# Attention of the first block: values stationary in two column halves, sums of weights by GpSimd and ones, results by feature

## The chip, the core and the metric

The kernel runs on one core of one Trainium2 chip. The core has five engines that run side by side and meet by semaphores: TensorE (matrix products, results in PSUM, eight banks of 128 partitions by 512 4-byte floats), VectorE, ScalarE, GpSimd (which reads and writes SBUF alone) and SyncE, which issues transfers. The metric is the time of one execution in microseconds (us) on the device; less is better.

## The reference, cut to what matters

The program is a block with retention and sparse attention, then a second block of two layers, in 4-byte floats, 512 tokens, width 1024. The change touches only the sparse attention of the first block. It has 8 query heads in 2 groups of 4 that share keys and values of 64 features, and three sides: compressed keys (31), selected keys and keys in a window. With 512 tokens the 16 best key blocks are all of the 8 that exist, so the second side takes in every earlier token, as the third does. For each block of 128 queries:

```python
p_cmp = masked_softmax(jnp.einsum('bgrtd,bgnd->bgrtn', qb, kc_g), valid_c)
o_cmp = jnp.einsum('bgrtn,bgnd->bgrtd', p_cmp, vc_g)
...
p_slc = masked_softmax(s_slc, smask).reshape(B, G, R, QB, topk, SLC_BLOCK)
o_slc = jnp.einsum('bgrtks,bgtksd->bgrtd', p_slc, vg)
...
p_win = masked_softmax(jnp.einsum('bgrtd,bgsd->bgrts', qb, kwb), wmask)
o_win = jnp.einsum('bgrts,bgsd->bgrtd', p_win, vwb)
...
out = gates[:, :, 0] * to_bshd(o_cmp) + gates[:, :, 1] * to_bshd(o_slc) + gates[:, :, 2] * to_bshd(o_win)
```

The result stands beside the retention's and is multiplied by the output projection.

## The kernel before

The stage has eight **units** (list `nsa`): four tiles `qt` of 128 queries by two groups `g`. A unit has one **block** of compressed keys (`s=0`) and two (`s=1, 2`) for each tile `kt` of 128 keys up to its own, 3, 5, 7 or 9 blocks, 48 in all. `first` is the number of a unit's first block, counted over all units.

For a block, `block_scores` writes scores of 128 keys by 4 heads x 128 queries into PSUM bank 4 or 5: a product of the high parts, a mask (compressed block and last key tile), a product with the rest parts, which also subtracts the largest score. ScalarE turns them into weights, `pr`, in a ring of four buffers. `block_values` then takes each head's 128x128 weights as the stationary operand and moves 65 columns of values, of which the last is one, so that the sum of the weights comes with the products. A product of plain 4-byte floats is two records of TensorE in the trace, one of the marked type (fp32r) is one. The sums of a unit's 12 heads and sides stand by token in banks 6 and 7.

The largest scores come from **rounds** (`best_round`): for the unit two further on, TensorE multiplies queries and keys in banks 2 and 3 in turn, VectorE reduces each over the keys (`largest`), `lowest` makes the shifts, `turn_low` transposes them in bank 1, and `spread_low` puts them among the rest queries `ql`. A round must wait until the one two before it is reduced.

At a unit's end VectorE (`unit_result`) bounds the sums, divides by them times the gates (`gates` holds one plus an exponential, so a division is the gate), multiplies all 12 results (`term`), and adds the three sides into `by_token`. After two units (one token tile) `turn_tokens` transposes four 128x128 tiles into bank 0 or 2, ScalarE writes the high part (`tokens_high`), VectorE the rest (`tokens_low`), in `h_hi` and `h_lo`, tiles 4 to 7. There is no scheduler: each engine runs its instructions in the order in which its function writes them. In the last two units TensorE also multiplies four tiles for the retention (`ret_widen`, its diagonal by `ret_diagonal` and its end by `ret_finish` on VectorE). VectorE splits two weight panels (`low(OUT1)`, `low(OUT1 + 1)`) before unit 5's results. ScalarE's halves of these splits (`split(33)`, `split(34)`) stand ahead of the first exponential.

After the stage the output projection takes tiles 0 to 3 (retention) of two panels, then tiles 4 to 7 (attention) of them: 24 and 24 products of 512 columns. GpSimd has nothing in the stage. A later attention of the kernel, in the second block (records L986 and L999, additions L588 on GpSimd, transposes L2696 on VectorE), works on two heads at a time in the two column halves of the array.

## Time and profile before

| | |
|---|---|
| median of 3 runs | 1913.14 us (1908.67 to 1914.05) |
| profiled execution | 1912.61 us |
| its span, first to last instruction | 1910.8 us |
| TensorE busy | 1856.8 us, 97% |
| VectorE, ScalarE, GpSimd busy | 1139.7, 735.9, 175.7 us |
| mean granted clock of TensorE | 0.991 |

"Busy" of TensorE counts each matmul to its modelled end, which lies beyond the start of the next; distances between starts tell more. A row of the timeline gives start, duration, engine, line, operation, operands, shapes and, in brackets, the idle time before it and what ended it. The granted clock is 1.00 at 2.4 GHz and 0.50 at 1.2 GHz.

### The profile page before, as it was taken

The numbers are of one execution on the slowest core, as the hardware profiler recorded it, in microseconds if no ns is written. First come the engines' busy times: TensorE is split into PE (matmuls) and PEld (weight loads), VectorE is DVE, ScalarE is ACT, GpSimd is POOL, SyncE is SP. The second block draws the span as 40 slices with busy tenths as digits, with TensorE's granted clock in tenths as the row PEclk, the third lists the DMA queues.
The fourth block names the chain that finished last, engine by engine and source line by source line (L and its number), as shares of the span: only waits on it lengthen the run. The fifth ranks groups of instructions, "written<-read, shape, count | busy, mean of one in ns | idle before, by whom it ended". The sixth has DMA issues, their size and how long they took to land.

```text
span 1910.8 us, 24681 instructions
## 1 busy us (share of the span) xinstructions
PE 1856.8 (97%) x8914; PEld 1513.4 (79%) x8914; DVE 1139.7 (60%) x1625; ACT 735.9 (39%) x1077; POOL 175.7 (9%) x181
## 2 busy tenths in 40 slices
PE   8999989999999999999999999999999999999998
PEld 6788778888888887887788888888666688888887
DVE  7767654784774778777543434476777554334344
ACT  6355222542432444554432322343544342323232
POOL 0020000300000011010000000002467300000000
PEclk9999999999999999999999999999999999999999
DMA  6232013233333332311333333332110133333332
GB/s 211 89 126 73 1 44 112 66 95 95 98 90 107 91 120 78 100 56 45 94 91 97 99 99 94 93 98 88 56 32 25 45 89 99 99 99 92 95 99 88
DMA packets 48216, 165.68 MB, mean 87 GB/s; under 512 B 5376, under 2 KB 7424, under 8 KB 48000
## 3 DMA queue, kind: packets, MB, share of 16 engines
q1 hardware_dynamic: 46512, 161.27, 27.8%
q10 hardware_dynamic: 1616, 3.22, 0.5%
q8 instruction: 56, 0.92, 0.2%
q14 instruction: 32, 0.26, 0.0%
HBM read 162.38 MB, written 2.10 MB: 86 GB/s over the span
## 4 chain that ended last, share of the span: by engine, by line
PE 86%; DVE 8%; ACT 2%; issue 2%; POOL 1%; DMA 0%; SPq 0%; DVEq 0%; ACTq 0%; POOLq 0%
PE ps L625 26%; PE ps L627 25%; PE ps L626 25%; PE ps L883 2%; PE ps L986 2%; DVE w_lo L2077 1%; POOL x L538 1%; ACT w_hi L1441 1%; PE ps L847 1%; PE ps L1241 1%; DVE tmp L2114 1%; PE ps L956 1%; PE ps L868 0%; DVE qk_c L2799 0%; PE ps L816 0%
## 5 line engine op out<-in xcount | busy, mean ns | idle before, releaser
L1441 ACT ACTIVATE w_hi<-raw 128x1024 fp32r<-128x1024 f32 x280 | 296.7, 1060 | 779.5 <-PE ps L627 779.3
L625 PE MATMUL ps<-h_hi,w_hi 128*128 128x512 f32 (+1 forms) x1288 | 509.3, 395 | 10.1 <-DVE w_lo L2352 7.2
L626 PE MATMUL ps<-h_lo,w_hi 128*128 128x512 f32 (+1 forms) x1288 | 500.0, 388 | 0.0
L627 PE MATMUL ps<-h_hi,w_lo 128*128 128x512 f32 (+1 forms) x1288 | 499.9, 388 | 0.0
L2077 DVE TENSOR_TENSOR w_lo<-raw,w_hi 128x1024 fp32r<-128x1024 f32 x280 | 345.0, 1232 | 120.6 <-ACT w_hi L1441 119.0
L625 PEld LDWEIGHTS ps<-h_hi,w_hi 128*128 128x128 f32 x1288 | 243.2, 189 | 64.6 <-DVE w_lo L2352 7.2
L627 PEld LDWEIGHTS ps<-h_hi,w_lo 128*128 128x128 f32 x1288 | 243.0, 189 | 50.6
L626 PEld LDWEIGHTS ps<-h_lo,w_hi 128*128 128x128 f32 x1288 | 243.1, 189 | 49.5 <-issue 2.0
L625 PE MATMUL ps<-hid_hi,w_hi 128*128 128x512 f32 (+1 forms) x716 | 273.6, 382 | 1.8 <-DVE w_lo L2077 0.9
L627 PE MATMUL ps<-hid_hi,w_lo 128*128 128x512 f32 (+1 forms) x716 | 272.6, 381 | 0.0
L626 PE MATMUL ps<-hid_lo,w_hi 128*128 128x512 f32 (+1 forms) x716 | 272.6, 381 | 0.0
L2292 DVE TENSOR_TENSOR x<-x,ps 128x512 f32<-128x512 f32 (+2 forms) x82 | 55.3, 674 | 191.6 <-PE ps L627 191.4
L625 PEld LDWEIGHTS ps<-hid_hi,w_hi 128*128 128x128 f32 x716 | 134.6, 188 | 28.9 <-DVE w_lo L2077 2.1
L627 PEld LDWEIGHTS ps<-hid_hi,w_lo 128*128 128x128 f32 x716 | 134.6, 188 | 25.9
L626 PEld LDWEIGHTS ps<-hid_lo,w_hi 128*128 128x128 f32 x716 | 134.6, 188 | 25.7
L2990 DVE SCALAR_TENSOR_TENSOR ev<-ps,tmp 128x512 f32<-128x512 f32 x64 | 44.1, 691 | 155.8 <-PE ps L627 152.8
L511 POOL TENSOR_TENSOR r<-r,small 128x2 f32<-128x2 f32 x6 | 4.2, 700 | 887.1 <-DVE r L2181 887.1
L1736 ACT ACTIVATE pr<-ps 128x512 f32<-128x512 f32 x48 | 27.9, 599 | 76.7 <-PE ps L873 76.6
L506 POOL TENSOR_TENSOR r<-r,small 128x4 f32<-128x4 f32 x8 | 8.1, 1012 | 516.2 <-DVE r L2127 516.2
L2684 DVE TENSOR_REDUCE mla_negm<-ps 128x1 f32<-128x512 f32 x64 | 41.2, 685 | 15.5 <-PE ps L956 14.8
L2732 DVE TENSOR_TENSOR ev<-ps,tmp 128x512 f32<-128x512 f32 x44 | 30.4, 692 | 28.8 <-PE ps L627 27.3
L625 PE MATMUL ps<-w_hi,h_hi 128*128 128x512 f32 (+1 forms) x128 | 47.0, 367 | 0.1
(412 smaller groups left out, 2522.8 us busy)
## 6 DMA issues: line engine op xcount, KB each, us to landing
raw<-in_panels SPq DMA_DIRECT2D x295, 512.0 KB, 3.6
x_in<-in_x SPq DMA_DIRECT2D x8, 256.0 KB, 5.7
x<-in_x ACTq DMA_DIRECT2D x1, 2048.0 KB, 8.4
out<-y SPq DMA_DIRECT2D x16, 128.0 KB, 1.8
first<-in_first SPq DMA_DIRECT2D x1, 1568.0 KB, 11.5
raw<-in_panels SPq DMA_DIRECT2D x2, 256.0 KB, 4.5
second<-in_second ACTq DMA_DIRECT2D x1, 512.0 KB, 3.7
small<-in_small ACTq DMA_DIRECT2D x1, 328.0 KB, 4.0
```

Of the source, the lines that this page charges most:

```text
L625: nc.tensor.matmul(out, a[0], b[0], start=start, stop=False)
L626: nc.tensor.matmul(out, a[0], b[1], start=False, stop=False)
L627: return nc.tensor.matmul(out, a[1], b[0], start=False, stop=stop)
L883: last = nc.tensor.matmul(ps[:, 6 + n // 6, n % 6 * 65:n % 6 * 65 + 65], pr[:, m % 4, h * P:(h + 1) * P], v, start=w["kt"] == 0 and n in ( ...
L986: last = nc.tensor.matmul(ps[64 * a:64 * a + 64, pair_bank(p), cols_of(half)], mla_v[:, kt, n, :], weights_tile(n, kt)[:, cols_of(half)], ...
L1441: nc.scalar.activation(w_high(panel, i), raw[:, panel % 4, :], ACT.Copy).then_inc(w_hi_ready, 1)
L1736: nc.scalar.activation(pr[:, m % 4, :], ps[:, 4 + m % 2, :], ACT.Exp, scale=0.125).then_inc(block_exp, 1)
L2077: signal(V.tensor_tensor(w_low(panel, i), raw[:, panel % 4, :], w_high(panel, i).bitcast(F32), ALU.subtract), w_lo_ready, wait=False)
L2292: signal(V.tensor_tensor(x[:, k, at], x[:, k, at], bank, ALU.add), done)
L2684: signal(V.tensor_reduce(mla_negm[:, n % 2, t:t + 1], ps[:, 2 + t % 2, :], AX.X, ALU.max, negate=True), mx_done, wait=False)
L2732: signal(V.tensor_tensor(src, bank, inv_b, ALU.mult), tile_out)
L2990: signal(V.scalar_tensor_tensor(ev[:, k % 4, :], bank, 0.0, inv_b, ALU.max, ALU.mult), tile_out, wait=False)
```

## The change

The values (64 columns now) become the stationary operand, and a block's weights move: heads 0 and 1 (256 columns) through the array's first 64 columns, heads 2 and 3 through the other 64. The result stands by feature, features of two heads in the two halves of 128 partitions. The compressed side goes to bank 0, the two others to bank 6 or 7 by unit. The rows of `w_out` are put in the order that fits, on the host's side.

The sums of weights come in another way. For the compressed block, `block_values` also multiplies its weights by ones. For the other sides GpSimd adds the weights of all key tiles (`add_block`), and `unit_sums` multiplies the totals by ones, in bank 1. The gates are spread once (`spread_gates`). VectorE has two functions for results: `compressed_result`, and `unit_result` for the other two sides; each transposes the sums in 32x32 squares, takes the larger of them and a bound times the gate value, the reciprocal, transposes back, and multiplies. GpSimd adds the three terms (`unit_add`) and, after ScalarE's rounding (`unit_rounded`), subtracts (`unit_rest`). For the last unit VectorE does both (`last_sum`). The transposes by token go.

The order is one list of 48 blocks, taken in pairs: the scores of two blocks (with their rounds), then the value products of the two before them; the sums of unit n come after the pair that holds block 2 of unit n+1. `pr` has six buffers. ScalarE's splits of the two panels go to unit 5, VectorE's to units 6 and 7. `x` is still loaded when ScalarE is through with the stage.

```diff
-            pr = sb("pr", [P, 4, S], F32, cc)
-            by_token = sb("by_token", [P, 2, 4, P], F32, cc)
-            term = sb("term", [P, 3, 4, 64], F32, cc)
+            pr = sb("pr", [P, PROBS, S], F32, cc)
+            term = sb("term", [P, 2, 3, 256], F32, cc)
+            unit_out = sb("unit_out", [P, 2, 256], F32, cc)
...
+        def add_block(m):
+            u, b = flat[m]
+            n, w = u["n"], u["blocks"][b]
+            if w["s"] == 0 or w["kt"] == 0:
+                return
+            if w["kt"] == 1 and n >= 2:
+                pool.wait_ge(unit_totals, n)
+            pool.wait_ge(block_exp, m + 1)
+            total = block_sum(n, w["s"])
+            nc.gpsimd.tensor_tensor(total, prob(m - 2) if w["kt"] == 1 else total, prob(m), ALU.add).then_inc(unit_added, 1)
+            pool.wait_ge(unit_added, last_add(m))
+        def unit_add(n):
+            pool.wait_ge(sum_taken, n + 1)
+            pool.wait_ge(compressed_taken, n + 1)
+            if n >= 2:
+                pool.wait_ge(unit_low, n - 1)
+            t = unit_out[:, n % 2, :]
+            nc.gpsimd.tensor_tensor(t, term[:, n % 2, 0, :], term[:, n % 2, 1, :], ALU.add).then_inc(unit_sum, 1)
+            pool.wait_ge(unit_sum, 2 * n + 1)
+            nc.gpsimd.tensor_tensor(t, t, term[:, n % 2, 2, :], ALU.add).then_inc(unit_sum, 1)
+            pool.wait_ge(unit_sum, 2 * n + 2)
...
+        def unit_rest(n):
+            pool.wait_ge(unit_high, n + 1)
+            hi, lo = unit_tiles(h_hi, nsa[n]), unit_tiles(h_lo, nsa[n])
+            nc.gpsimd.tensor_tensor(lo, unit_out[:, n % 2, :].rearrange("p (j q) -> p j q", j=2), hi.bitcast(F32), ALU.subtract).then_inc(unit_low, 1)
+            pool.wait_ge(unit_low, n + 1)
...
+        for m in range(NSA_BLOCKS):
+            for u in nsa[1:]:
+                if m == u["first"] + 5:
+                    unit_add(u["n"] - 1)
+            add_block(m)
+            for u in nsa[1:]:
+                if m == u["first"] + 10:
+                    unit_rest(u["n"] - 1)
+        unit_rest(NSA_UNITS - 2)
...
+        def unit_sums(u):
+            n = u["n"]
+            if u["qt"]:
+                pe.wait_ge(unit_added, adds_before[n + 1])
+            pe.wait_ge(unit_taken, bank_one["taken"])
+            pe.wait_ge(low_spread, bank_one["spread"])
+            for s in (1, 2):
+                moving = block_sum(n, s) if u["qt"] else prob(u["first"] + s)
+                for a in range(2):
+                    last = nc.tensor.matmul(ps[64 * a:64 * a + 64, 1, cols_of(s - 1)], ones[:, 0:64], moving[:, cols_of(a)],
+                                            start=True, stop=True)
+            last.then_inc(unit_totals, 1)
+            bank_one["taken"] = n + 2
...
+            if b == 0 and n:
+                pe.wait_ge(compressed_taken, n)
+            if b == 0 and n == NSA_UNITS - 1:
+                pe.wait_ge(mix_ready, 2)
+            if b == 1 and n >= 2:
+                pe.wait_ge(sum_taken, n - 1)
-            for h in range(4):
-                n = 4 * w["s"] + h
-                last = nc.tensor.matmul(ps[:, 6 + n // 6, n % 6 * 65:n % 6 * 65 + 65], pr[:, m % 4, h * P:(h + 1) * P], v,
-                                        start=w["kt"] == 0 and n in (0, 6), stop=w["last"], skip_group_check=True)
+            bank, at = (6 + n % 2, cols_of(w["s"] - 1)) if w["s"] else (0, cols_of(0))
+            for a in range(2):
+                last = nc.tensor.matmul(ps[64 * a:64 * a + 64, bank, at], v, prob(m)[:, cols_of(a)], start=w["kt"] == 0 and w["s"] < 2,
+                                        stop=w["last"], skip_group_check=True)
+            if b == 0:
+                for a in range(2):
+                    last = nc.tensor.matmul(ps[64 * a:64 * a + 64, 0, cols_of(1)], ones[:, 0:64], prob(m)[:, cols_of(a)], start=True,
+                                            stop=True, skip_group_check=True)
...
-        for n, u in enumerate(nsa):
-            count = len(u["blocks"])
-            block_scores(u, 0)
-            block_scores(u, 1)
-            if n + 1 < NSA_UNITS:
-                turn_low(nsa[n + 1])
-            block_values(u, 0)
-            if n and n % 2 == 0:
-                turn_tokens(n // 2 - 1)
-            for b in range(1, count):
-                if b + 1 < count:
-                    block_scores(u, b + 1)
-                if n + 2 < NSA_UNITS:
-                    for r in rounds_at(n, b):
-                        best_round(nsa[n + 2], r)
+        for m in range(2):
+            block_scores(*flat[m])
+        turn_low(nsa[1])
+        for m in range(0, NSA_BLOCKS, 2):
+            for k, (u, b) in enumerate(flat[m:m + 2]):
+                if m + 2 + k < NSA_BLOCKS:
+                    block_scores(*flat[m + 2 + k])
+                if u["n"] + 2 < NSA_UNITS:
+                    for r in rounds_at(u["n"], b):
+                        best_round(nsa[u["n"] + 2], r)
+            for u in nsa[2:]:
+                if m == turned_at(u["n"]):
+                    turn_low(u)
+            for u, b in flat[m:m + 2]:
                 block_values(u, b)
+            if m == 0:
+                spread_gates()
+            for u, b in flat[m:m + 2]:
+                n = u["n"]
+                if b == 2 and n:
                 if n >= NSA_UNITS - 2 and b in (2, 5):
-                    if n == NSA_UNITS - 2 and b == 2:
-                        pe.wait_ge(mix_ready, NT - 1)
+                    pe.wait_ge(compressed_taken, n + 1)
                     ret_widen(2 * (n - NSA_UNITS + 2) + b // 3)
-        turn_tokens(NT - 1)
+        unit_sums(nsa[-1])
...
+        for m in range(NSA_BLOCKS):
+            act.wait_ge(block_s, m + 1)
+            if m >= PROBS:
+                u, b = flat[m - PROBS]
+                act.wait_ge(block_pv, m - PROBS + 1)
+                if last_add(m - PROBS):
+                    act.wait_ge(unit_added, last_add(m - PROBS))
+                elif b:
+                    act.wait_ge(unit_totals, u["n"] + 2)
+            nc.scalar.activation(prob(m), ps[:, 4 + m % 2, :], ACT.Exp, scale=0.125).then_inc(block_exp, 1)
+            for u in nsa[1:]:
+                if m == u["first"] + 8:
+                    unit_rounded(u["n"] - 1)
+            if m in (nsa[-3]["first"] + 2, nsa[-3]["first"] + 4):
+                split(OUT1 + (m - nsa[-3]["first"]) // 2 - 1)
...
+        def compressed_result(u):
+            n, w = u["n"], w24[:, 0:8]
+            totals, shares = tmp[:, 1, 0:256], tmp[:, 1, 256:S]
+            dve.wait_ge(block_pv, u["first"] + 1)
+            link(V.transpose(totals, ps[:, 0, 256:S]))
+            link(V.scalar_tensor_tensor(w, totals[:, 0:256:32], 1e-30, gate_at(u, 0, 1)[:, 0, :], ALU.max, ALU.mult))
+            link(V.reciprocal(w, w))
+            link(V.transpose(shares, w.unsqueeze(2).to_broadcast([P, 8, 32])))
+            if n >= 2:
+                dve.wait_ge(unit_sum, 2 * n - 2)
+            signal(V.tensor_tensor(term[:, n % 2, 2, :], ps[:, 0, 0:256], shares, ALU.mult), compressed_taken, wait=False)
...
         def unit_result(u):
-            n, g, qt = u["n"], u["g"], u["qt"]
-            by = ps[:, 6:8, 0:390].rearrange("p b (i d) -> p b i d", d=65)
-            halves = w12[:].rearrange("p (b i) -> p b i", b=2)
-            sides = w12[:].rearrange("p (s h) -> p s h", s=3)
+            n, w = u["n"], w24[:, 8:24]
+            totals, shares = sq[:, 0, :], sq[:, 1, :]
+            dve.wait_ge(unit_totals, n + 2)
+            signal(V.transpose(totals, ps[:, 1, :]), unit_taken)
+            link(V.scalar_tensor_tensor(w.rearrange("p (s c) -> p s c", s=2), totals[:, 0:S:32].rearrange("p (s c) -> p s c", s=2), 1e-30,
+                                        gate_at(u, 1, 3), ALU.max, ALU.mult))
+            link(V.reciprocal(w, w))
+            link(V.transpose(shares, w.unsqueeze(2).to_broadcast([P, 16, 32])))
             dve.wait_ge(block_pv, u["first"] + len(u["blocks"]))
...
+        V.tensor_scalar(gates[:, :, 0:24], gates[:, :, 0:24], 1e38, 1.0, ALU.min, ALU.add).then_inc(gates_ready, 1)
+        spread_low(nsa[1])
+        for m in range(0, NSA_BLOCKS, 2):
+            for u, b in flat[m:m + 2]:
+                if u["n"] + 2 < NSA_UNITS:
+                    for r in rounds_at(u["n"], b):
+                        largest(nsa[u["n"] + 2], r)
+                    if b == len(u["blocks"]) - 1:
+                        lowest(nsa[u["n"] + 2])
+            for u in nsa[2:]:
+                if m == turned_at(u["n"]):
+                    spread_low(u)
...
+            for u, b in flat[m:m + 2]:
+                n = u["n"]
+                if b == 0:
+                    compressed_result(u)
+                if b == 2 and n:
+                    unit_result(nsa[n - 1])
+                if n == NSA_UNITS - 2 and b == 1:
+                    ret_diagonal(0)
-            if n + 2 < NSA_UNITS:
-                lowest(nsa[n + 2])
-            if n == NSA_UNITS - 3:
-                ret_diagonal(0)
-                low(OUT1)
-                low(OUT1 + 1)
+                if n >= NSA_UNITS - 2 and b == 7:
+                    low(OUT1 + n - NSA_UNITS + 2)
```

The start of unit 4 on TensorE, before (`kcs`, `ks` keys, `qs` queries, `vc`, `nv` values, `negm` shifts):

```order
L868 MATMUL ps<-qs0,kcs0 128x512 [waits block_exp,low_spread]
L871 MATMUL ps<-masks 128x512
L873 MATMUL ps<-ql0,kcl0 128x512
L868 MATMUL ps<-qs0,ks00 128x512 [waits block_exp,low_spread]
L873 MATMUL ps<-ql0,kl00 128x512
L859 MATMUL ps<-small,negm 12x128 [waits low_spread,low_ready]
L883 MATMUL ps<-vc,pr 128x65 [waits sum_taken,block_exp]
L883 MATMUL ps<-vc,pr 128x65 x3
```

and now, from the scores of its third block on:

```order
L960 MATMUL ps<-qs0,ks00 128x512 [waits block_exp,low_spread]
L965 MATMUL ps<-ql0,kl00 128x512
L910 MATMUL ps<-ks00,qs0 128x512 [waits best_done]
L914 MATMUL ps<-masks 128x128
L979 MATMUL ps<-pr,vc 64x256 [waits compressed_taken,block_exp]
L979 MATMUL ps<-pr,vc 64x256
L983 MATMUL ps<-pr,small 64x256 x2
L979 MATMUL ps<-pr,nv 64x256 [waits sum_taken,block_exp]
L979 MATMUL ps<-pr,nv 64x256
```

The first value products now stand behind the scores of two further blocks, they no longer wait for the unit before (`compressed_taken` is of unit 3's first block, `sum_taken` of unit 2), and two blocks' products are together.

The results of unit 3 on VectorE, before:

```order
L2607 TENSOR_SCALAR negm<-mx 128x12 [waits best_done]
L2624 TENSOR_SCALAR w<-ps 128x12 [waits block_pv]
L2625 TENSOR_TENSOR w<-w,gates 128x12 [waits dve_step]
L2626 RECIPROCAL w<-w 128x12 [waits dve_step]
L2627 TENSOR_TENSOR term<-ps,w 128x768 [waits dve_step]
L2632 TENSOR_TENSOR by_token<-term 128x4x64 [waits sum_taken]
L2633 TENSOR_TENSOR by_token<-by_token,term 128x4x64 [waits dve_step]
```

and now, with the compressed results of unit 4 ahead of them and reductions (L2706) between:

```order
L2731 STREAM_TRANSPOSE tmp<-ps 128x256 [waits block_pv]
L2732 SCALAR_TENSOR_TENSOR w<-tmp,gate_w 128x8 [waits dve_step]
L2733 RECIPROCAL w<-w 128x8 [waits dve_step]
L2734 STREAM_TRANSPOSE tmp<-w 128x256 [waits dve_step]
L2737 TENSOR_TENSOR term<-ps,tmp 128x256 [waits unit_sum,dve_step]
L2706 TENSOR_REDUCE mx<-ps 128x1 [waits best_ready] x3
L2719 TENSOR_TENSOR ql<-ps,small 12x512 [waits low_turned]
L2744 STREAM_TRANSPOSE sq<-ps 128x512 [waits unit_totals]
L2745 SCALAR_TENSOR_TENSOR w<-sq,gate_w 128x16 [waits unit_taken]
L2747 RECIPROCAL w<-w 128x16 [waits dve_step]
L2748 STREAM_TRANSPOSE sq<-w 128x512 [waits dve_step]
L2752 TENSOR_TENSOR term<-ps,sq 128x512 [waits unit_sum,block_pv,dve_step]
```

One set of results became two, each with two transposes, and reductions stand behind both.

GpSimd's last instructions in the stage, where it had none (`ev` holds the totals):

```order
L561 TENSOR_TENSOR ev<-pr 128x512 [waits block_exp,unit_totals,unit_added]
L571 TENSOR_TENSOR unit_out<-term 128x256 [waits compressed_taken,unit_low,sum_taken,unit_added]
L573 TENSOR_TENSOR unit_out<-unit_out,term 128x256 [waits unit_sum]
L561 TENSOR_TENSOR ev<-ev,pr 128x512 [waits block_exp,unit_sum]
L561 TENSOR_TENSOR ev<-ev,pr 128x512 [waits block_exp,unit_added] x3
L580 TENSOR_TENSOR h_lo<-unit_out,h_hi 128x2x128 [waits unit_high,unit_added]
```

Unit 6's results stand ahead of the last four additions of unit 7, for which TensorE's last sums wait.

## Rows read from the trace of the kernel before

**Rows 1.** page, part 4: chain that ended last, shares by engine.

```profile
PE 86%; DVE 8%; ACT 2%; issue 2%; POOL 1%; DMA 0%; SPq 0%; DVEq 0%; ACTq 0%; POOLq 0%
```

**Rows 2.** busy time by engine in windows: units 0+1, 2+3, 4, 5, 6, 7.

```profile
core 0: us, PE busy (x) PEld busy (x) DVE busy (x) ACT busy (x) POOL busy (x), PEclk, DMA share, GB/s
177.10:194.10 17.00, 15.62 (x116) 12.75 (x116) 11.21 (x25) 3.93 (x7) 0.00 (x0) 1.00 0.00 1
194.10:218.30 24.20, 22.51 (x161) 18.01 (x161) 16.00 (x36) 6.23 (x12) 0.00 (x0) 1.00 0.01 2
218.30:233.30 15.00, 14.39 (x102) 11.46 (x103) 9.22 (x19) 4.58 (x9) 0.00 (x0) 1.00 0.00 0
233.30:252.40 19.10, 15.62 (x98) 12.25 (x98) 11.60 (x21) 4.07 (x7) 0.00 (x0) 0.91 0.08 24
252.40:270.00 17.60, 16.95 (x102) 14.33 (x102) 10.31 (x19) 5.72 (x10) 0.00 (x0) 0.90 0.09 35
270.00:286.80 16.80, 14.08 (x96) 12.04 (x97) 8.91 (x17) 4.21 (x8) 0.00 (x0) 1.00 0.19 65
```

**Rows 3.** groups of lines by form, 160 to 300 us: | busy us, mean ns | idle, releaser.

```profile
L883 PE MATMUL ps<-vc,pr 128*128 128x65 f32 x64 | 9.0, 284 | 7.1 <-DVE term L2627 5.9 <-ACT pr L1736 1.2
...
L2627 DVE TENSOR_TENSOR term<-ps,w 128x768 f32<-128x768 f32 x8 | 7.7, 957 | 0.3
...
L2632 DVE TENSOR_TENSOR by_token<-term 128x256 f32<-128x256 f32 x8 | 3.4, 425 | 0.3
...
L2642 DVE TENSOR_TENSOR h_lo<-ps,h_hi 128x512 fp32r<-128x512 f32 x4 | 2.7, 686 | 4.2 <-ACT h_hi L1727 4.2
```

**Rows 4.** timeline of TensorE, two plain blocks of unit 6.

```profile
260.25 0.48 PE L868 MATMUL ps<-qs,ks 128*128 128x512 f32 x1
260.57 0.40 PE L873 MATMUL ps<-ql,kl 128*128 128x512 f32 x1
260.81 1.00 PE L883 MATMUL ps<-nv,pr 128*128 128x65 f32 x8
261.61 0.47 PE L868 MATMUL ps<-qs,ks 128*128 128x512 f32 x1
```

**Rows 5.** timeline of TensorE, column halves in the later attention.

```profile
1408.62 1.08 PE L999 MATMUL ps<-tmp,small 128*64 128x256 f32 x8 [0.30 <-issue]
1409.50 0.38 PE L986 MATMUL ps<-c_raw,mla_v 128*64 128x256 f32 x1
...
1411.05 0.38 PE L986 MATMUL ps<-ev,mla_v 128*64 128x256 f32 x1
1411.36 0.50 PE L625 MATMUL ps<-q_hi,k_hi 128*128 128x512 f32 x1
1411.70 0.40 PE L626 MATMUL ps<-q_lo,k_hi 128*128 128x512 f32 x1
...
1416.27 0.61 PE L956 MATMUL ps<-k_hi,q_hi 128*128 128x512 f32 x2
1416.82 0.43 PE L986 MATMUL ps<-c_raw,mla_v 128*64 128x256 f32 x1
```

**Rows 6.** timelines of TensorE and VectorE: starts of units 3 and 6, the end.

```profile
206.36 0.41 PE L883 MATMUL ps<-vc,pr 128*128 128x65 f32 x2 [0.50 <-DVE term L2627]
...
248.40 2.36 DVE L2077 TENSOR_TENSOR w_lo<-raw,w_hi 128x1024 fp32r<-128x1024 f32 x2
...
252.44 0.41 PE L883 MATMUL ps<-vc,pr 128*128 128x65 f32 x2 [3.50 <-DVE term L2627]
...
286.40 0.66 PE L891 MATMUL ps<-small,by_token 128*128 128x128 f32 x4 [2.72 <-DVE by_token L2633]
```

**Rows 7.** groups by form, whole span, GpSimd and VectorE.

```profile
L538 POOL TENSOR_TENSOR x<-x,tmp 128x256 f32<-128x256 f32 x32 | 26.9, 870 | 6.4 <-DVE tmp L2196 6.3
L588 POOL TENSOR_TENSOR tmp<-tmp,c_raw 128x512 f32<-128x512 f32 x16 | 23.8, 1485 | 5.1 <-ACT c_raw L1717 4.2
...
L2696 DVE STREAM_TRANSPOSE sq<-ps 128x512 f32<-128x512 f32 x8 | 5.7, 717 | 6.0 <-PE ps L999 5.9
```

149 lines of the change are left out of this document (79 added, 70 removed).

## The prediction

> **What bounds the kernel now.** I read the chain of work that ended last first: 86% of the span is TensorE's [rows 1], so a microsecond counts only where TensorE works or waits. The change touches one stage, the block attention from 177.1 to 286.8 us. The windows by unit [rows 2] show TensorE busy in most of each unit, but that figure hides short waits, since a matmul's shown duration overlaps the next one's. So I work from distances between starts. VectorE is busy 67.3 us in the six windows (11.2 + 16.0 + 9.2 + 11.6 + 10.3 + 8.9), ScalarE 28.7 us, GpSimd not at all. The stage is TensorE's, with VectorE second, and TensorE waits for VectorE in places that can be named [rows 6]. The granted clock is 1.00 but in two windows, 0.91 over 19.1 us and 0.90 over 17.6 us [rows 2]: some 3.5 us at the lower of its two levels (1.2 for 2.4 GHz) in each, the second behind a wait of 3.5 us [rows 6]. Each cost half of that, 1.7 us.
>
> **Products of a block.** Now four heads' weights are each the stationary operand and 65 columns of values move: eight records (each product in 4-byte floats is two). From one block's scores (260.25) to the next one's (261.61) is 1.36 us: 0.32 to the second score product, 0.24 to the first value product, 0.80 to the next scores [rows 4]. There are 48 blocks in 24 pairs, so a pair of unmasked ones takes 2.72 us. The new form has no row in this stage, but a later attention of this kernel uses it: 64 columns stationary, 256 moving, the two column halves alternating. Eight such records, which is what two blocks will need, take 0.88 us (1408.62 to 1409.50), and the return to full-width products costs 0.31 and then 0.34 us between starts, where 0.24 is usual [rows 5]. Entering costs 0.32 (1416.27 has two records in the list, so I take 0.55 from the first, less one usual step of 0.23) [rows 5]. A new pair: 0.34 + 0.24 + 0.24 for its four score products, 0.32 to enter, 0.67 from the first to the last of eight value records (sixteen take 1.55, 1409.50 to 1411.05, less 0.88), 0.31 to leave: 2.12 us. That saves 0.60 a pair, 14.4 us for 24. The bounds: without the switching cost (0.26 a pair, namely 0.10 + 0.08 + 0.08 over usual steps) 20.6 us; if each block of a pair paid it, 8.2 us.
>
> The page TensorEngine Tiling (Array Packing) of the Trainium skill (section Key Properties) says that changing the tiling mode, not merely the tile, drains the engine, and it speaks against this change. By that rule, the trace agrees: 0.31 and 0.34 us on the way out [rows 5]. With it the products save 14.4 us, without it 20.6.
>
> **What TensorE gets in addition.** Sums of weights no longer come with a 65th column. Per unit: four records with ones for the compressed block, half of 0.88, and eight for the two summed sides, 0.88. Eight units: 3.5 + 7.0 = 10.5 us [rows 5]. Once, the gates are spread with eight records of 96 columns, at the 0.11 us of a record of 65 (0.80/7) [rows 4] 0.9 us; at twice that 1.8. What goes: four times four transposes, at 0.11 us a record as well, 1.8 us. TensorE's own work falls by 14.4 - 10.5 - 0.9 + 1.8 = 4.8 us. That is small: most of the gain must come from waits.
>
> **Waits that go.** At each unit's start TensorE issues two score blocks and the turned shifts, and then stands before the first value products, for the exponential of a block scored just before and for the old sums to be read. The group of those products has 7.1 us of idle time before it, 5.9 of it put down to the reading of the old sums and 1.2 to the exponential [rows 3]; the ordinary case is the 0.50 at 206.36, the worst the 3.50 at 252.44, where VectorE had first split two weight panels (2.36 us) [rows 6]. The new order takes the value products of two blocks after the scores of the next two, across units, and results are read two blocks later; banks 6 and 7 alternate by unit. So both causes go. The splits of the two panels stand in units 6 and 7 now. ScalarE's two splits ahead of the first exponential go too, and a copy of one 128x512 tile comes: two splits of over 1 us against about 0.6, of which I count 0.7, since VectorE is behind there. The half clock: one of two windows follows the 3.5 us wait that goes, 1.7 us back; the other I leave.
>
> **What is late next.** (1) VectorE. A unit's results are now two sets. The compressed one: two 32x32 block transposes of 256 columns (half of 0.717 each, at least), two small operations, one product of 0.425 [rows 3, 7], about 1.9 us with gaps. The other: two transposes at 0.717, two small operations, a product at 0.686, 2.7 us. Before: 0.957 + two of 0.425 + three small ones, 2.4 us. That is +2.2 us a unit, or 17 for eight, less the four subtractions of 0.686 that go to GpSimd, +15 us: VectorE's 67 become 82 us busy, with 0.04 us before each dependent operation (0.3 for eight of L2632 [rows 3]) and some 150 operations 88. TensorE's stage falls to near that. In units 0 and 1 VectorE has ten of its reductions, three results, gates and a shift, some 15 us in the 17.0 of [rows 2], so these hardly shorten. TensorE may be two score rounds ahead of the reductions (two banks), so a third round in a pair must wait behind a result. I count 1.5 us for that, between 0 and the 27.6 us of a rival below.
> (2) GpSimd. It adds the weights: two additions for each key tile after the first, 24 in all, at the 1.48 us mean of the same addition later in the kernel [rows 7]; per unit also two additions and a subtraction of 256 columns at 0.870. In the last units that is 6 x 1.48 + 3 x 0.87 = 11.5 us and handshakes, in units of some 13 us: it keeps up, and ScalarE, which has six weight buffers instead of four and now waits for the additions too, isn't held. Only at the very end is it late. From the last results of unit 6 two additions of 256 and the last four of 512 columns follow each other: 1.7 + 5.9 + handshakes of some 0.6 = 8.2 us, after about 2.9 for VectorE's results, 11.1. TensorE has to do 8 us from the same moment (one diagonal product 0.9, a plain pair 2.1, a masked pair with another diagonal 3.6, two value products 1.2). So it waits some 3 us, where it waits 2.72 now [rows 6], and then issues the 0.88 of sums already counted. I add 0.4 us. The output projection's first half (24 records of 0.23, 5.5 us) covers the 4.9 us of the last results on VectorE.
> The longer masks, score products and rounds don't change, and nothing later than the stage does. Weights for the next panels are split later, at units 6 and 7, but are wanted only after 286 us; cover 10 us or more.
>
> The page GPSIMD Engine Reference of the Trainium skill (section Specifications) says that GpSimd shares its SBUF interfaces with VectorE, with contention when VectorE reads two SBUF inputs. In the later attention VectorE was busy too, and the same additions took 1.48 us [rows 7]; whether this stage's mix is worse no row here shows. If it is, rival E is what happens.
>
> **Sum.** -4.8 (work) - 7.1 (unit starts) - 0.7 (first exponential) - 1.7 (clock) + 1.5 (rounds behind results) + 0.4 (end) = -12.4 us. The profiled execution took 1912.6 us (span 1910.8 and 1.8 around it), 0.5 under the median of 1913.1. So 1912.6 - 12.4 + 0.5 = 1900.7 us.
>
> **The rivals.**
> A, more than the sum: TensorE never waits for VectorE and both half clocks go. Then 1.5 and 1.7 more and switching costs little (up to 3): 1895. For it: the later attention of this kernel has such pairs and no half clock there. Against: VectorE's load comes within 2 us of TensorE's.
> B, VectorE sets the stage: it has 88 us without any waiting, and each wait for a first value product delays it. In the six windows it now sits idle 42 of 109.7 us. If 13 to 15 us of that stay, plus the end, the stage is 105: gain 5 us, 1908. For it: reductions and results alternate on one queue.
> C, slower: the results stand in front of the rounds in each unit that has rounds (0 to 5). If TensorE stood for all of both sets, 1.9 + 2.7 us in six units, 27.6 us come on top instead of 1.5: 1927. It decides from the point where over half of that is exposed. Against: a pair gives TensorE 2 us or more of other work, and only the third round of a pair is bound.
> D, the halves don't overlap and the change doesn't do what it says: 72 further groups of 0.43 us (48 blocks, 8 compressed sums, 16 unit sums), 31 us, 1932. Against: rows of the very form [rows 5].
> E, GpSimd sets the pace: at 2.1 us for an addition the last two units become 15.2 instead of 13 us each and the end 2.5 later: gain 5, 1908.
>
> **How the numbers follow.** The sum's case (1897 to 1905) 0.53, A 0.16, B 0.17, E 0.06, C 0.06, D 0.02. About 0.3%, 5.7 us, is what a measurement of this kernel can tell from no change: faster means under 1907.4. Faster: the sum and A, and near half of B and E, 0.79. Same: most of the rest, 0.14. Slower: C and D with their surroundings, 0.07. The range takes A's and B's ends: 1893 to 1909.
>
> **What would show it.** Value products of a pair in eight records over 0.88 us, with 0.31 + 0.34 after them; no wait of over 1 us at a unit's start; VectorE's transposes at 0.72 and 0.4; GpSimd's additions at 1.3 to 1.5; the last sums of TensorE waiting some 3 us for GpSimd; stage length near 98 us; at most two half-clock windows in and just behind the stage. I am wrong if rounds wait for reductions by more than 5 us in total, or ScalarE waits for additions in the middle of the stage.

## The result, and the profile after

The changed kernel is slower by a little: 1915.03 us median of 20 runs (1911.75 to 1919.6) against 1910.68 of 20 runs of the kernel before (1908.53 to 1915.48), a ratio of 1.0022 (95% interval 1.0015 to 1.0030). The forecast was 1900.7, in a range of 1893 to 1909, and stood on the median of 3 runs of before, 1913.14. A gain of 12.4 us was expected and a loss of 4.3 was found.

The profiled execution of after took 1912.69 us (span 1910.0), at the low end of its runs; that of before stands in the upper third of its own, with 6.8 us at half clock ahead of the stage that after's lacks. The spans alone would hide the loss. From the first score product to the first product of the output projection the stage takes 112.1 us before (174.75 to 286.82) and 116.8 after (171.34 to 288.11), 4.7 us more.

That figure is too high by 1.5 us, because before has a lowered stretch just behind this end, where its wait of 2.72 us stood, and after has hardly any. The first row is the window behind the stage in before; the two others are the thirteenth product of the projection, before and after.

```profile
286.82:290.20 3.38, 3.38 (x12) 2.68 (x11) 0.69 (x1) 0.60 (x1) 0.00 (x0) 0.55 0.78 299
291.24 0.39 PE L625 MATMUL ps<-h_hi,w_hi 128*128 128x512 f32 x1
291.02 0.39 PE L688 MATMUL ps<-h_hi,w_hi 128*128 128x512 f32 x1
```

Counted from the first score product to this one, the change costs 119.7 - 116.5 = 3.2 us in these two executions. The medians differ by 4.3, the fastest runs by 3.2.

The chain that ended last, part 4 of the page, answers [rows 1]: VectorE's share has grown from 8 to 10%.

```profile
PE 84%; DVE 10%; ACT 2%; issue 2%; POOL 1%; DMA 0%; SPq 0%; DVEq 0%; ACTq 0%; POOLq 0%
```

Busy time of after by unit (units 0+1, 2+3, 4, 5, 6, 7, each from its first value product), answering [rows 2]. The columns are window, its length, then busy us and count of each engine, and the granted clock.

```profile
176.10:193.90 17.80, 15.79 (x112) 10.33 (x110) 13.37 (x31) 3.55 (x6) 0.74 (x2) 1.00 0.00 0
193.90:221.60 27.70, 24.06 (x137) 13.89 (x136) 18.88 (x41) 6.27 (x12) 10.17 (x11) 0.91 0.00 1
221.60:235.40 13.80, 13.38 (x79) 7.58 (x80) 10.53 (x21) 4.71 (x10) 5.58 (x6) 0.93 0.00 1
235.40:250.70 15.30, 13.42 (x80) 7.19 (x76) 10.56 (x20) 5.77 (x10) 9.00 (x9) 1.00 0.01 2
250.70:270.80 20.10, 14.65 (x74) 7.34 (x75) 16.97 (x23) 5.42 (x11) 12.45 (x10) 0.92 0.00 1
270.80:288.10 17.30, 14.10 (x76) 6.80 (x72) 14.26 (x21) 3.91 (x8) 11.32 (x10) 0.91 0.42 152
```

Units 6 and 7 now have VectorE busy for 31.2 of 37.4 us, against 19.2 of 34.4 in [rows 2], while TensorE is busy for 28.8. Four windows, not two, carry a lowered clock. Time lost to it: 27.7 x 0.09 + 13.8 x 0.07 + 20.1 x 0.08 + 17.3 x 0.09 = 6.6 us, against 3.5 in [rows 2]. Cut closer, the same view has three places:

```profile
212.00:225.00 13.00, 11.57 (x54) 6.84 (x52) 7.06 (x16) 2.96 (x6) 3.45 (x4) 0.74 0.00 0
262.00:270.00 8.00, 5.89 (x20) 2.84 (x20) 6.48 (x8) 1.55 (x4) 4.99 (x4) 0.79 0.00 1
282.00:289.00 7.00, 5.36 (x22) 2.60 (x23) 5.58 (x6) 0.00 (x0) 4.80 (x4) 0.76 0.77 291
```

That is 6.8 us (216.6 to 223.4), 3.4 (from 264.4) and 3.4 (from 284.9) at the lower level.

What TensorE waits for inside the stage, from the view of waits (line, releaser, total us, times, longest):

```profile
PE ps L891 <- DVE tmp L2689: 8.6, 3, 4.9
PE ps L910 <- DVE mx L2706: 5.9, 7, 1.5
```

The first is the product that spreads the retention's roots over the partitions: it waits for the tile of diagonals that VectorE builds. The second is a score round that waits for a reduction. In [rows 3, 6] the longest waits were at the units' first value products and at the end. The place of the worst, VectorE and GpSimd side by side in the timeline of unit 6:

```profile
255.58 0.70 DVE L2744 STREAM_TRANSPOSE sq<-ps 128x512 f32<-128x512 f32 x1
...
257.57 0.69 DVE L2752 TENSOR_TENSOR term<-ps,sq 128x512 f32<-128x512 f32 x1
258.30 0.75 DVE L2696 SCALAR_TENSOR_TENSOR tmp<-ro,small,ps 128x512 f32<-128x512 f32 x1
259.08 0.69 DVE L2698 TENSOR_TENSOR tmp<-tmp,rg 128x512 f32<-128x512 f32 x1
259.80 0.83 DVE L2194 CAST h_hi<-tmp 128x512 fp32r<-128x512 f32 x1
260.67 1.63 DVE L2195 TENSOR_TENSOR h_lo<-tmp,h_hi 128x512 fp32r<-128x512 f32 x1
262.33 1.63 DVE L2689 TENSOR_TENSOR tmp<-small,ret 128x512 f32<-128x512 f32 x1
...
260.43 4.67 POOL L561 TENSOR_TENSOR ev<-ev,pr 128x512 f32<-128x512 f32 x3
...
264.11 1.76 PE L891 MATMUL ps<-tmp,small 128*128 128x512 f32 x2 [4.93 <-DVE tmp L2689]
```

VectorE runs without a gap: unit 5's results, then one head of the retention (four operations), then the next diagonal. Two of them take 1.63 us, while GpSimd adds three times. Seven microseconds later the same subtraction takes 0.69. It starts 0.07 us ahead of GpSimd's next addition, and this time the addition is the longer one, 1.76 us:

```profile
267.88 0.69 DVE L2195 TENSOR_TENSOR h_lo<-tmp,h_hi 128x512 fp32r<-128x512 f32 x1
267.95 1.76 POOL L561 TENSOR_TENSOR ev<-ev,pr 128x512 f32<-128x512 f32 x1 [2.86 <-ACT pr L1838]
```

The groups by form, whole stage, answer [rows 3, 7]:

```profile
L561 POOL TENSOR_TENSOR ev<-ev,pr 128x512 f32<-128x512 f32 x12 | 17.2, 1431 | 3.7 <-ACT pr L1838 2.9
L561 POOL TENSOR_TENSOR ev<-pr 128x512 f32<-128x512 f32 x12 | 15.3, 1274 | 22.2 <-ACT pr L1838 19.6 <-DVE term L2737 2.3
...
L2689 DVE TENSOR_TENSOR tmp<-small,ret 128x512 f32<-128x512 f32 x4 | 6.5, 1628 | 0.1
...
L2744 DVE STREAM_TRANSPOSE sq<-ps 128x512 f32<-128x512 f32 x8 | 5.7, 714 | 6.7 <-PE ps L948 6.7
...
L2195 DVE TENSOR_TENSOR h_lo<-tmp,h_hi 128x512 fp32r<-128x512 f32 x4 | 4.7, 1165 | 0.1
L2731 DVE STREAM_TRANSPOSE tmp<-ps 128x256 f32<-128x256 f32 x8 | 3.6, 450 | 6.4 <-PE ps L983 6.4
```

GpSimd's additions and VectorE's transposes take what was forecast. What the prediction had not priced are the diagonal and the retention's h_lo (two of its four at 1.63 us, two at 0.69). The products themselves came out as forecast; TensorE at the end of unit 5, answering [rows 4, 5]:

```profile
248.62 1.08 PE L979 MATMUL ps<-pr,nv 128*64 128x256 f32 x8
249.63 0.50 PE L960 MATMUL ps<-qs,ks 128*128 128x512 f32 x1
249.97 0.40 PE L965 MATMUL ps<-ql,kl 128*128 128x512 f32 x1
250.20 0.40 PE L960 MATMUL ps<-qs,ks 128*128 128x512 f32 x1
250.44 0.40 PE L965 MATMUL ps<-ql,kl 128*128 128x512 f32 x1
250.76 0.44 PE L979 MATMUL ps<-pr,vc 128*64 128x256 f32 x2
```

Eight value records and the way out take 1.01 us, the four score products 0.34 + 0.23 + 0.24, the way in 0.32: 2.14 us for a plain pair.

### The profile page after: what moved, and what is told of

It is laid out like the page before. It is cut to its first block, busy times and chain, and to the rows that moved or that the text cites. A ratio compares the mean times of both kernels' runs of the same rounds, so it can differ in the third digit from the quotient of the medians.

```text
span 1910.0 us, 24626 instructions
## 1 busy us (share of the span) xinstructions
PE 1851.1 (97%) x8810; PEld 1483.5 (78%) x8810; DVE 1162.1 (61%) x1658; ACT 737.2 (39%) x1082; POOL 225.0 (12%) x226
## 4 chain that ended last, share of the span: by engine, by line
PE 84%; DVE 10%; ACT 2%; issue 2%; POOL 1%; DMA 0%; SPq 0%; DVEq 0%; ACTq 0%; POOLq 0%
PE ps L688 25%; PE ps L690 25%; PE ps L689 25%; PE ps L1079 2%; DVE w_lo L2182 1%; POOL x L601 1%; PE ps L979 1%; ACT w_hi L1542 1%; DVE tmp L2219 1%; PE ps L910 1%; PE ps L1049 1%; PE ps L1342 1%; DVE qk_c L2934 0%; PE ps L960 0%; PE ps L1092 0%
```

## The experiments

The theory from this profile: TensorE's side of the forecast is right, and VectorE takes it back, by the longer results, by slower operations beside GpSimd's additions, and by the order in which diagonals and reductions stand behind results. The rival: TensorE's own products, their changes between column halves and full width, and its clock set the stage. All ratios are to the kernel before, which was run again beside each group of experiments (its medians were 1910.7 to 1912.4). Differences to after are between ratios, 0.0005 being 1 us. With intervals of some 0.0012 either way, a difference of 2 us or less says nothing. Several results lay outside what I had written for either theory (the two with results later, the load of 24 additions, all three edits together); they are reported with the rest.

**The retention's slots.** Do the diagonals only stand in a bad place?

```diff
+RET_AT = ((6, 5), (6, 7), (7, 3), (7, 5))
...
-                if n >= NSA_UNITS - 2 and b in (2, 5):
+                if (n, b) in RET_AT:
```

> The changed kernel with the four retention diagonals and ends moved from blocks 2 and 5 of the last two units to blocks 5 and 7 of unit 6 and 3 and 5 of unit 7, so that none stands behind unit results on VectorE. In the changed kernel TensorE waited 4.9 and 3.1 us for a diagonal. Theory 1 (the gain was lost to diagonals and rounds that stand behind VectorE's results): 5 to 8 us faster than the changed kernel, near 1908. Theory 2 (VectorE has too much to do in the stage, wherever it stands): the wait only moves, under 2 us faster, 1913 or more.

1915.04 us, ratio 1.0023 (1.0011 to 1.0035): nothing. The waits stayed, 8.5 us in two.

```profile
PE ps L892 <- DVE tmp L2690: 8.5, 2, 4.4
```

The diagonal is built behind the head before it, wherever both stand, so a slot later the same chain is late.

**Results later.** The order of VectorE's queue: all results of units 0 to 5 one pair later.

```diff
+            results_of(m - 2 if m - 2 <= RESULTS_LATE else NSA_BLOCKS)
             for u in nsa[2:]:
...
-                if b == 0:
-                    compressed_result(u)
-                if b == 2 and n:
-                    unit_result(nsa[n - 1])
```

> The changed kernel with VectorE's two result functions taken one pair of blocks later, behind the next pair's reductions, in units 0 to 5. Theory 1: TensorE's rounds no longer wait behind results (some 8 us of such waits in the changed kernel), 4 to 7 us faster than it, near 1910. Theory 2: VectorE's sum of work is the same, so under 1.5 us faster.

1923.0 us, 1.0055 (1.0036 to 1.0074), some 6 us worse than after. With the retention's slots as well:

> Both moves together, the retention's and the results'. Theory 1: the two gains add up, 10 to 14 us faster than the changed kernel, 1901 to 1905, faster than before by 0.3 to 0.5%. Theory 2: 3 us at most, 1912.

1922.94 us, 1.0062 (1.0045 to 1.0078). In the first of the two the reductions' waits nearly went (1.3 us in one), but TensorE now stood for the shifts and the bank of the sums (5.7 us), for the shifts' transposes (3.0) and still for diagonals (5.4; 4.1 with the slots moved too). With the compressed results alone moved:

```diff
+            for u in nsa[0:6]:
+                if u["first"] // 2 * 2 + 2 == m:
+                    compressed_result(u)
...
-                if b == 0:
+                if b == 0 and n >= 6:
                     compressed_result(u)
```

> The changed kernel with only the compressed result (five VectorE instructions, 2.3 us) of units 0 to 5 moved one pair of blocks later, behind that pair's reductions; the results of units stay. TensorE waited 1.25, 1.08, 0.91, 1.40 and 1.86 us for a reduction at the pair behind such a result, 6.5 us. Theory (these waits are time on the path): 1909 to 1912. Theory load (VectorE's sum sets the units, as moving both kinds of results later made it slower): within 1.5 us of the changed kernel's 1915, or more.

1920.51 us, 1.0042 (1.0027 to 1.0056): 4 us worse than after, against the theory of waits. VectorE and TensorE inside unit 2:

```profile
205.27 0.44 DVE L2731 STREAM_TRANSPOSE tmp<-ps 128x256 f32<-128x256 f32 x1
...
207.00 0.71 DVE L2744 STREAM_TRANSPOSE sq<-ps 128x512 f32<-128x512 f32 x1
...
209.79 0.69 DVE L2752 TENSOR_TENSOR term<-ps,sq 128x512 f32<-128x512 f32 x1
210.52 1.02 DVE L2706 TENSOR_REDUCE mx<-ps 128x1 f32<-128x384 f32 x2
...
211.13 0.28 PE L910 MATMUL ps<-kcs,qs 128*128 128x32 f32 x1 [2.00 <-DVE mx L2706]
```

In after the compressed result of that unit was done before the pair's reductions, VectorE then stood idle for 1.33 us ahead of unit 1's result, and the same round waited 0.74 us. A pair later the two results stand together: ten operations in front of the reduction. At unit 1 the next compressed product also waits 2.29 us for the one bank. "Later" moved work from an idle slot into a full one.

**Switching.** Value products of each block on their own, 24 more changes of width.

```diff
+                if k == 0:
+                    block_values(u, b)
...
-            for u, b in flat[m:m + 2]:
-                block_values(u, b)
+            block_values(*flat[m + 1])
```

> The changed kernel with the value products of each block on their own, the first block's right behind the next scores, instead of two blocks together: 24 more switches to column halves and back. If a switch costs TensorE the 0.26 us read from the later attention and TensorE sets the time, 6 us slower than the changed kernel, 1921. If VectorE sets the time of the stage, the products cost nothing there: within 1.5 us of it, 1915 or a little less.

1914.63 us, 1.0015 (1.0004 to 1.0027). Twenty-four more changes cost nothing at the end of the chain, where the rival asked for 6 us. The edit also gives the first block's products earlier, and the waits for reductions shrank (1.9 us instead of 5.9), so it isn't the number of changes alone. Together with the run on VectorE's load below, it speaks against the rival: TensorE's products don't set the stage.

**GpSimd's additions**, cut to 8 of 512 columns in units 4 to 7 of the changed kernel (20 of the 24, so that most of these sums are left out), and then added to the kernel before.

```diff
+            c = S if n < 4 else 8
-            nc.gpsimd.tensor_tensor(total, prob(m - 2) if w["kt"] == 1 else total, prob(m), ALU.add)
+            nc.gpsimd.tensor_tensor(total[:, 0:c], (prob(m - 2) if w["kt"] == 1 else total)[:, 0:c], prob(m)[:, 0:c], ALU.add)
```

> The changed kernel, but GpSimd's additions of weights in units 4 to 7 (20 of the 24) cover 8 of their 512 columns; the denominators from unit 4 on are therefore incomplete. Every instruction, wait and semaphore stays, only GpSimd's time in them goes (about 1.3 to 1.7 us each down to some tenths). Theory contention (VectorE's operations that read two SBUF tiles are slowed by GpSimd's additions): the diagonals (128x512, small times ret) fall from 1.63 to about 0.69 us, h_lo of the retention from 1.17 to 0.69, TensorE's waits for the diagonal shrink by some 2 to 4 us, and the kernel takes about 1910 to 1912, 3 to 5 us below the changed kernel. Theory order (the diagonals and results are late because of what stands ahead of them on VectorE, whatever GpSimd does): VectorE's durations may fall, the time stays within 1 us of 1915.

1908.58 us, 0.9988 (0.9977 to 0.9998), 6.5 us below after. The groups: the diagonal at 0.80 us in the mean instead of 1.63, h_lo at 0.69. TensorE waits for diagonals 4.5 us in two instead of 8.6 in three.

```profile
L2690 DVE TENSOR_TENSOR tmp<-small,ret 128x512 f32<-128x512 f32 x4 | 3.2, 800 | 0.1
...
L2196 DVE TENSOR_TENSOR h_lo<-tmp,h_hi 128x512 fp32r<-128x512 f32 x4 | 2.8, 692 | 0.1
```

The other way round, in the kernel before:

```diff
+                if w["s"] and w["kt"]:
+                    pool.wait_ge(block_exp, u["first"] + b + 1)
+                    nc.gpsimd.tensor_tensor(ev[:, w["s"] - 1, :], ev[:, w["s"] - 1, :], ev[:, w["s"] + 1, :], ALU.add)
```

> The kernel before, plus 24 additions 128x512 on GpSimd (SBUF to SBUF, on a tile that nothing of the stage reads), one behind each block's exponential for which the changed kernel has one. Nobody waits for them. Contention: the kernel before shows the slow durations that the changed one has (the diagonal 1.63 instead of 0.69 us, retention's h_lo 1.17 instead of 0.69, w_lo above 1.4 instead of 1.22), some 4 to 8 us more on VectorE, of which 1 to 4 us reach the end: 1912 to 1915. If GpSimd's additions don't slow VectorE by themselves: durations and time stay those of the kernel before, 1910.7 within 0.6.

1920.88 us, 1.0048 (1.0030 to 1.0067): 9 us, for 24 additions that no other engine waits for. That is over twice what I had expected at most. In its trace the stage takes 8.8 us more. Waits for diagonals and at the end make up 4.9; the rest is lowered clock (0.94 over the stage, 0.97 before), part of it behind the wait of 3.5 us that the kernel before has too. The timelines:

```profile
263.64 1.55 DVE L2101 CAST h_hi<-tmp 128x512 fp32r<-128x512 f32 x1
265.22 1.65 DVE L2102 TENSOR_TENSOR h_lo<-tmp,h_hi 128x512 fp32r<-128x512 f32 x1
266.90 1.64 DVE L2596 TENSOR_TENSOR tmp<-small,ret 128x512 f32<-128x512 f32 x1
271.41 0.43 DVE L2101 CAST h_hi<-tmp 128x512 fp32r<-128x512 f32 x1
271.87 0.69 DVE L2102 TENSOR_TENSOR h_lo<-tmp,h_hi 128x512 fp32r<-128x512 f32 x1
...
263.63 4.35 POOL L538 TENSOR_TENSOR ev<-ev 128x512 f32<-128x512 f32 x3 [2.91 <-ACT pr L1748]
271.95 1.76 POOL L538 TENSOR_TENSOR ev<-ev 128x512 f32<-128x512 f32 x1 [3.96 <-ACT pr L1748]
```

The cast, with one SBUF input, is slowed too (0.43 to 1.55). The subtraction at 271.87, which starts 0.08 us ahead of an addition, keeps its 0.69, and that addition takes 1.76. The diagonal waits appear in this kernel, which had none, 4.6 us in two. With the additions in units 2 to 5 only:

> The kernel before plus GpSimd's additions 128x512 in units 2 to 5 only (12 of the 24 of the run with all of them, which cost 9 us). In these units VectorE reduces scores from PSUM and multiplies from PSUM; only two operations from SBUF with two inputs stand in each unit, of 256 columns. Contention by two SBUF inputs: the reductions stay at 0.69, 1910 to 1913, nearly all of the 9 us is in units 6 and 7. If the additions cost by something else (power and clock, semaphores, ScalarE): 1915 to 1917, half of the 9 us.

1910.7 us, 0.9994 (0.9981 to 1.0008). Twelve additions at 1.27 us cost nothing where VectorE reads PSUM; its reductions keep their 688 ns:

```profile
L2613 DVE TENSOR_REDUCE mx<-ps 128x1 f32<-128x512 f32 x16 | 10.5, 688 | 9.5 <-PE ps L863 9.5
```

So the contention costs in units 6 and 7, where the retention is SBUF to SBUF. In units 2 to 5 no cost can be measured; the two weight splits there, which read two SBUF tiles, kept their 1.22 us and so met no addition.

**Repairs.** Two tiles for the diagonals, each built a slot ahead:

```diff
-            nc.tensor.matmul(ps[:, 0, :], ones, tmp[:, 3, :], start=True, stop=True)
+            nc.tensor.matmul(ps[:, 0, :], ones, tmp[:, 3 - h % 2, :], start=True, stop=True)
...
                     ret_diagonal(0)
+                    ret_diagonal(1)
...
-                    if h < 3:
-                        ret_diagonal(h + 1)
+                    if h < 2:
+                        ret_diagonal(h + 2)
```

> The changed kernel with two tiles for the retention's diagonals, so that each is made one slot earlier than its widening product needs it, ahead of the results of units 6 and 7, and TensorE no longer waits for it (8.6 us in three waits). Nothing is left out. Theory wait (these waits are time on the path): about 1909 to 1911, 4 to 6 us less than the changed kernel. Theory VectorE (units 6 and 7 are set by the sum of VectorE's work, the diagonal is only where it shows): the wait moves to the retention's results, to the exchange of banks or to the last results, and the time is 1913 to 1915.5.

1913.96 us, 1.0000 (0.9989 to 1.0012), 4 us below after. Part of the wait moved to the head before it, which must have read the bank, and another 1.9 us to the last sums, which now stand for GpSimd:

```profile
PE ps L893 <- DVE h_lo L2197: 5.3, 2, 3.9
```

Sums of units 6 and 7 by ones behind each block's values, in the rounds' banks:

```diff
+            if w["s"] and n >= BY_ONES:
...
+                for a in range(2):
+                    last = nc.tensor.matmul(ps[64 * a:64 * a + 64, 2 + n % 2, at], ones[:, 0:64], prob(m)[:, cols_of(a)],
+                                            start=w["kt"] == 0 and w["s"] < 2, stop=w["last"], skip_group_check=True)
```

> The changed kernel, but in units 6 and 7 no weights are added by GpSimd: the sums over keys are products with ones behind each block's values, accumulated in the banks of the score rounds, which are free by then (16 blocks, about 0.45 us of TensorE each, less the two separate sums, some +5.5 us of products); complete result. If GpSimd's additions are what makes VectorE late at the end of the stage (retention's diagonals at 1.63 instead of 0.69 us, h_lo 1.17 to 1.63 instead of 0.69), VectorE gets 5 to 7 us back there, its waits cover the added products, and the kernel takes 1908 to 1912. If TensorE's own work sets these two units, it takes 1917 to 1921.

1912.09 us, 1.0002 (0.9990 to 1.0014), 4 us below after although TensorE has more to do: its added products fit into its waits (for a diagonal it stands 2.5 us in one, instead of 8.6). Both repairs:

> Both repairs of the end of the stage together: diagonals one slot ahead in two tiles, and sums of units 6 and 7 by ones instead of GpSimd. If they act on the same wait (VectorE too late in units 6 and 7), the gain is little more than that of the better one alone: 1908 to 1911. If they add up: 1904 to 1908.

1911.43 us, 0.9996 (0.9981 to 1.0010). 5 us together, where 4 and 4 stood alone: most likely one wait for the most part, VectorE late in the last two units, though the intervals don't rule out two separate losses. All three edits:

> The three edits together: diagonals ahead, sums of units 6 and 7 by ones, compressed results of units 0 to 5 one pair later. Nothing is left out. If the lost gain is the three named losses (diagonal waits, contention with GpSimd in the last units, rounds behind compressed results), this comes near the forecast for the changed kernel: 1901 to 1906. If VectorE's load as such sets the stage: 1908 to 1912.

1914.62 us, 1.0013 (1.0001 to 1.0026): the compressed results a pair later cost 3 us here too.

**VectorE's load.** The results of units 2 to 7 on 32 columns:

```diff
+            c = 32 if n >= 2 else 256
...
-            link(V.transpose(totals, ps[:, 0, 256:S]))
+            link(V.transpose(totals[:, 0:c], ps[:, 0, 256:256 + c]))
```

> The changed kernel, but VectorE's work on the results of units 2 to 7 covers one group of 32 columns (the two 32x32 block transposes and the product with the shares, of 256 and 512 columns before): the result tiles of these units are incomplete. That takes about 6 x (2 x 0.35 + 0.3) + 6 x (2 x 0.6 + 0.55), some 16 us, from VectorE and nothing from TensorE; the number of instructions and waits stays. Theory VectorE (its longer results, in front of reductions, shifts and diagonals, took the expected gain): the kernel falls by 6 to 12 us, to 1903 to 1909. Theory other (TensorE's own products and its clock set the stage, VectorE is beside them): no more than 2 us less than the changed kernel.

1906.27 us, 0.9975 (0.9964 to 0.9986), 9 us below after; it leaves most of these results out. And with GpSimd's short additions too:

> The changed kernel with both reductions of work at once: VectorE's results of units 2 to 7 on 32 columns, and GpSimd's additions of units 4 to 7 on 8 of 512 columns (results and denominators of those units incomplete). Alone they took 9 and 6.5 us off the changed kernel. If they are two separate losses: 1899 to 1902, which is the forecast of the changed kernel. If both act on the same waits (VectorE late in units 6 and 7): 1903 to 1906.

1898.33 us, 0.9943 (0.9921 to 0.9966), 15 us below after where the two alone give 6.5 and 9: they add up, within an interval of 4 us either way from five runs. The stage falls to 101.9 us (171.40 to 273.26); its one window, in the columns as above:

```profile
171.40:273.30 101.90, 94.11 (x576) 54.18 (x576) 68.71 (x161) 32.48 (x58) 27.45 (x45) 0.98 0.05 17
```

**One term alone in the kernel before.** The two weight splits and the first diagonal, ahead of unit 5's results in [rows 6], go to units 6 and 7:

```diff
+                if n == NSA_UNITS - 2 and b == 1:
+                    ret_diagonal(0)
+                if n >= NSA_UNITS - 2 and b == 7:
+                    low(OUT1 + n - NSA_UNITS + 2)
...
-            if n == NSA_UNITS - 3:
-                ret_diagonal(0)
-                low(OUT1)
-                low(OUT1 + 1)
```

> The kernel before with one piece of the change alone: the two splits of the output panels (w_lo, 2 x 1.22 us) and the first diagonal, which stood ahead of unit 5's results on VectorE, are taken in units 6 and 7 where the changed kernel has them. Complete result. If the wait of 3.0 us that TensorE had at the first value product of unit 6 is time on the path, and with it the clock's half-speed stretch behind it: 1906 to 1909. If VectorE is as late in units 6 and 7 instead, or the time is given back: 1910 to 1912.

1906.76 us, 0.9976 (0.9964 to 0.9988): 4.6 us faster than before and 9 faster than after, the fastest kernel here that leaves nothing out. At the place of the 3.50 us wait stands a shorter one:

```profile
252.56 1.08 PE L883 MATMUL ps<-vc,pr 128*128 128x65 f32 x8 [0.63 <-ACT pr L1736]
```

From the first score product to the thirteenth of the projection its trace shows 113.9 us against 116.5 before, 2.6 of the 4.6 us, though more of it runs at the lower clock in the stage (0.95 against 0.97).

## Why the prediction was wrong

**Products: right.** A plain pair takes 2.14 us where 2.12 was put. The page TensorEngine Tiling (Array Packing) of the Trainium skill (section Key Properties) says that a change of tiling mode drains the engine; the trace agrees, with 0.32 us on the way in and 0.34 behind the way out, where 0.23 is usual. But 24 more changes moved nothing at the end, since TensorE had waits to spare.

**Waits at the units' starts: right, and half of it not the change's own merit.** No first value product waits for a result. But about half of the 7.1 us was one wait of 3.50, and moving two splits and a diagonal in the kernel before takes it down to 0.63 and brings 4.6 us.

**"I count 1.5 us for that": too small.** In the view of waits seven rounds stand for a reduction, 5.9 us, five of them behind results (0.91, 0.89, 0.74, 1.43 and 1.51; from start to start, less the usual step, 6.3); before had four, 1.3 us. My own sign for being wrong, over 5 us, came true. The rival C had the right place and too high a price: about a fifth of its 27.6.

**"VectorE's 67 become 82 us busy": the step that failed.** The windows above show 84.6 us, and that it is so near to 82 is luck: two errors cancel. The count was too high, by 2.4 us for sets of results that take 1.74 and 2.55 us instead of 1.9 and 2.7, and by the last unit's 2.6, which fall behind the stage. Against that I had put every operation at its duration of before. Beside GpSimd the four diagonals take 6.5 us instead of 2.8, h_lo 4.7 instead of 2.8, the casts 2.9 instead of 1.7 and the splits 3.0 instead of 2.4, some 7.5 us in all. I had weighed the page GPSIMD Engine Reference of the Trainium skill (section Specifications), which says that the two engines contend when VectorE reads two SBUF inputs. By that rule, the trace agrees: 1.63 against 0.69 us. But I took GpSimd for the victim (rival E, additions at 2.1 us, 0.06), when its additions took 1.27 to 1.43 in the mean and VectorE's diagonals doubled. The row I leaned on, the same addition in a later attention at 1.48, says what happens to GpSimd and nothing of VectorE.

The second error is where the load stands: I divided a stage's sum by a stage's length. Units 6 and 7 hold the whole retention, the splits that the change moved there and half of the 24 additions; there VectorE is busy 31 of 37 us, and TensorE stands behind a chain of result, head and diagonal, 8.6 us in three waits. The prediction names the diagonals only as TensorE's work and puts the wait for them at nothing.

**The clock: wrong sign.** Instead of 1.7 us returned, more were lost: 6.6 against 3.5 in the stage, or 6.7 against 5.2 up to the thirteenth product of the projection, since before loses 1.7 just behind the stage. The prediction hadn't counted that third stretch. The lowered stretches of after begin 0.3 to 1.3 us behind the end of a wait (215.44, 264.11, 283.58). But one wait of 1.51 us (ending at 243.99) isn't followed by one, and the kernel with the two splits moved has the lower clock from 235.9 to 246.1 with no wait over 0.64 us ahead of it. So a wait may cost more than its length, but that waits bring the lowered stretches isn't shown. The stage with both loads cut shows 0.98 above, that of after 0.94.

**The end: better than forecast.** The last sums follow the last values at once (286.11), instead of 3 us for GpSimd. GpSimd had caught up since TensorE was late itself.

**The sum again.** Forecast -12.4, found +3.2 up to the thirteenth product, 15.6 apart: diagonals 8.6; rounds 5.9 less the 1.3 of before and the 1.5 counted, 3.1; clock 1.5 + 1.7 = 3.2; the end -3.1. That makes 11.8. The other 3.8 I can't put on single rows: there are many steps of 0.4 to 0.9 us, among them 0.87 for an exponential held up by the sums of unit 1. ScalarE stood there for products of TensorE, never for GpSimd's additions, so my second sign didn't come true.

**Was the forecast's other half right?** With VectorE's results cut and GpSimd's additions short, the kernel takes 12.5 us less than before by medians (10.9 by the ratio), and -12.4 was the forecast. That fits TensorE's terms; but this kernel does less on VectorE than the forecast granted it, and its interval is 4 us wide either way, so it isn't the forecast's kernel and no proof of each term. Rival B, VectorE sets the stage, was right in kind and 9 us too mild: it gave a gain of 5, and a loss of 4.3 came.

## What to carry to other kernels

Work that goes to an idle engine isn't free if it shares memory with a busy one: price the neighbour's operations, not only its own. Sum the second engine's load over the stretch that already holds most of it, and follow its longest dependent chain there, since a stage's mean hides both. Before a rewrite, take the largest single wait of the trace and ask what stands ahead of it; here two moved splits and a diagonal gave what the rewrite didn't.

## What was new on the hardware

- A GpSimd addition of 128x512 floats in SBUF that is already under way slows VectorE's 128x512 operations with two SBUF inputs from 0.69 to 1.63 us, and a cast with one from 0.43 to 1.55 at most. VectorE's reductions and products that read PSUM keep their 0.69 us.
- Where VectorE's subtraction started first, by 0.07 and 0.08 us (267.88 in the changed kernel, 271.87 in the kernel with 24 additions), it kept its 0.69 us and the addition took 1.76 instead of 1.27. So which of the two is slowed went by the order of their starts.
- Twenty-four such additions that no engine waits for cost 9 us in units 2 to 7, and twelve of them, in units 2 to 5, nothing that can be measured (interval up to 1.5 us).
- A small VectorE operation with two SBUF inputs (128x16) took 0.18 us with GpSimd idle (256.32 in the changed kernel) and 0.98 beside one of its additions, ending 0.03 us behind it (207.74 + 0.98 against 207.40 + 1.29), in the kernel with the compressed results late:

```profile
207.74 0.98 DVE L2745 SCALAR_TENSOR_TENSOR w<-sq,gate_w 128x16 f32<-128x16 f32 x1
...
207.40 1.29 POOL L561 TENSOR_TENSOR ev<-pr 128x512 f32<-128x512 f32 x1 [5.02 <-ACT pr L1838]
```
